# Tokens held step by step in a decoder step kernel, with the first GLU weights split in halves after the state-space loop

## The chip, the cores and the metric

One Trainium2 chip, one of its cores. The metric is the device time of one execution in microseconds (us). The engines are TensorE (PE, with its weight loads as PEld), VectorE (DVE), ScalarE (ACT), GpSimd (POOL) and SyncE (SP, which here only issues transfers).

## The reference

The kernel does one step of a two-layer decoder for 256 prompt tokens and 8 samples of 4 tokens each (288 tokens, width 1024). Layer 0 mixes with latent attention over a paged cache and gated linear attention, layer 1 with an S5 state-space layer. Cut to what the change touches:

```python
# layer 0
h = x + ab_mixer(rmsnorm(x, g_ab)) @ w_out            # residual add
h = h + squared_relu_mlp(rmsnorm(h, g_mlp0))
h = h + sigmoid(rmsnorm(h, g_ple0) @ w_gate) * (p0 @ w_proj)
# layer 1: S5
n = rmsnorm(h, g_c)                                   # "norm 3" in the kernel
u = n.reshape(l, 64 groups, 16)
x_t = lam * x_{t-1} + Bbar u_t                        # a complex state of 64 per group, scanned over t
y = Re(C x) + d * n
zg = gelu(y) @ w_glu
h = h + zg[:, :1024] * sigmoid(zg[:, 1024:])
h = h + squared_relu_mlp(rmsnorm(h, g_mlp1))
h = h + sigmoid(rmsnorm(h, g_ple1) @ w_gate) * (p1 @ w_proj)
```

## The kernel before

**Layout.** Activations lie transposed: channels on the partitions, the 288 tokens along the free dimension, in 8 blocks of 128 channels (`h3[:, b]` is block b of the residual `hT`, `n3` the normalised one). In the program before the tokens stand in their own order, prompt first and then the samples. The S5 layer works on 72 groups of TS = 4 consecutive tokens (J = 72, of which 64 are prompt and 8 are samples), so there every reader takes "step i of group j", which in this layout is every fourth token: `shifted` (L1137 to L1147), which puts the four steps of a block on four groups of 32 partitions, and the `permuted` add in `gated` (L1953).

**Precision.** Most weight matrices are split on the chip into two fp32r parts: ScalarE copies the high part (`hi_unit`, L1284), VectorE subtracts it from the weights to get the low part (`lo_unit`, L1632, 128x2048 elements), and the activations are split likewise (`n_hi_half` at L1557, `n_lo` at L1636). A block is then three matmuls (L750, L751, L752). The other matrices are multiplied in plain fp32 (L769). A unit of 2048 columns streams into a ring of five buffers.

**Order.** Every engine's order is written out by hand. `plan()` gives each PSUM result a bank; a result waits until all readers of the bank's last result are through. Four banks (0 to 3) are handed round to "main" results, four (4 to 7) to "side" results.

**The places of the change.** After the layer-0 MLP, `lag_products` makes the S5 kernel matrices `("G", 0..7)` in two groups of four, in one go; behind them stand the last two blocks (6, 7) of the sums of squares of norm 2. VectorE copies each G (L2055), ScalarE takes three shifted copies of it (L1507) after VectorE's. `ple(0)` follows: for each i of 8, `proj`, `gate` (16 instructions of L769), transposes `("BT", n)` of the S5 matrices (L1137), one block of the sums of squares of norm 3 (L724), and from i = 5 on `shifted(i - 5)` (L1146). When the last sum is there, ScalarE makes the reciprocal root (L1524 on 288 tokens, then L1527, four instructions that pick each step's 72 values for its 32 partitions), and VectorE scales the inputs by it (L2073).

Then the S5 loop, bound together over three engines: per i VectorE turns the inputs (L2085, L2086), scans (L2101), turns back (L2107) and writes the states (L2113, L2114); TensorE makes the inputs (L1192) and the outputs (L1200, and L1206 and L1207 once the states are there); ScalarE applies the GELU (L1550). Inside VectorE's loop, at its i = 6 and 7, stand the low parts that the GLU matrices need first:

```python
                if i == 6:
                    for b in range(4):
                        n_lo(2, b, glu_nhi)
                    lo_unit(U["glu0"])
                if i == 7:
                    lo_unit(U["glu1"])
```

TensorE's GLU begins with blocks 0 to 3 of units glu0 and glu1, then blocks 4 to 7 of both, then glu2 to glu7.

Of the kernel before, what the change touches and what calls it, by code (L numbers as in the profile page):

```python
# [20 lines left out]
P = 128  # L21
# [39 lines left out]
def lay(sizes):  # L61

    at, out = 0, {}
    for name, n in sizes:
# [18 lines left out]
                ("a2", FB * T), ("coef", 20 * 32), ("rsi", J)])  # L83
# [20 lines left out]
def turns(i):  # L104

    return range(3 * i, min(3 * i + 3, 16))


def plan():
# [88 lines left out]
    side("oa")  # L198
    for i in range(8):
        main(("out", i))  # L200
    for L in range(2):
        if L == 1:
            g.add(("ss", 3), "side", 4, 7)
# [26 lines left out]
        g.add(("ss", 2 + 3 * L), "side", 1, 7)  # L230
# [11 lines left out]
def program(nc, ins, outs):  # L242
    g = plan()
    ctx = ExitStack()
    with ctx:
# [59 lines left out]
        bc = lambda ap, shape: ap.broadcast_to(shape)  # L305

# [141 lines left out]
        rsi = s5("rsi")  # L448
# [4 lines left out]
        def sems(names):  # L453
# [12 lines left out]
         hi_ready, unit_split, n_hi, n_split, a_hi, a_split, p_hi, p_split, gate_ready, pool_step, rotation_ready, turned_back, d_ready, x_ready, samples_in, wfin_ready) = sems(  # L466
# [4 lines left out]
            "hi_ready unit_split n_hi n_split a_hi a_split p_hi p_split gate_ready pool_step rotation_ready turned_back d_ready x_ready samples_in wfin_ready")  # L471
# [71 lines left out]
        def _(sp):  # L543
# [28 lines left out]
            sp.wait_ge(table2_in, 16)  # L572
            sp.wait_ge(main_ready, g.of["kpss"][2])
# [131 lines left out]
        def _(pe):  # L705
# [14 lines left out]
            def sumsq_part(k, b):  # L720
# [3 lines left out]
                mm = pe.matmul(ps[:, 0:T], o1024, sq3[:, b % 4], start=b == 0, stop=b == DB - 1)  # L724
# [355 lines left out]
            def mlp(L):  # L1080
# [26 lines left out]
                lag_products()  # L1107
                sumsq_part(2, 6)
                sumsq_part(2, 7)

            def lag_products():
# [3 lines left out]
                for first in (0, 4):  # L1115
                    banks = [bank(("G", first + k)) for k in range(4)]
                    for s in range(4):
                        for bm, cm in ((Bre, Cre), (Bim, Cim)):
                            for k in range(4):
                                blk = 4 * (first + k) + s  # L1120
                                pe.matmul(banks[k][32 * k:32 * k + 32, P * s:P * s + P], bm[:, blk, 3], cm[:, blk, 0:4].rearrange("p i c -> p (i c)"),
                                          start=s == 0 and bm is Bre, stop=False, skip_group_check=True)
                    if first == 0:
                        pe.wait_ge(d_ready, 2)
                    for s in range(4):
                        for k in range(4):
                            mm = pe.matmul(banks[k][32 * k:32 * k + 32, P * s:P * s + 32], ident[0:32, 0:32], diag_d[0:32, 4 * (first + k) + s],
                                           start=False, stop=s == 3, skip_group_check=True)
                            if s == 3:
                                ready(mm, ("G", first + k))  # L1130
# [9 lines left out]
            def shifted(i):  # L1140
# [80 lines left out]
            def glu_pieces(i, lo, hi, wait=None):  # L1221

                w = split_unit(f"glu{i}")
# [7 lines left out]
            for i in range(2, 8):  # L1231
# [1092 lines left out]
```

## Time and profile before

| | |
|---|---|
| median of 3 runs | 1150.16 us (1148.03 to 1151.51) |
| profiled execution: its time / span in the trace | 1150.72 us / 1149.0 us |
| TensorE busy | 1065.5 us, 93% of the span |
| VectorE / ScalarE / GpSimd busy | 544.2 / 413.1 / 140.2 us |
| TensorE busy from 808.0 to 817.5 us | 0.43 us |
| mean granted clock of TensorE | 0.941 of full |

The span is what the trace shows between the first and the last instruction; the profiled execution's own time has 1.7 us around it. A granted clock of 1.00 is 2.4 GHz and 0.50 is 1.2 GHz. A busy TensorE is not one that is at its peak: its instructions overlap. Where it stands idle in the middle of the program, the engine that it waits for sets the time.

### The profile page before, as it was taken

The page shows a single profiled execution, that of the slowest core. Times are in us where ns is not written, and L with a number is a line of the kernel's source. Part 1 is how long each engine was busy: PE and PEld are TensorE (multiplying, and loading weights), DVE is VectorE, ACT ScalarE, POOL GpSimd, SP SyncE. Part 2 cuts the span into 40 slices and gives each one's busy share as a digit, 9 for nine tenths or more (in the row PEclk, how much of TensorE's full clock was granted, in tenths as well). Part 3 has the DMA queues.
Part 4 walks back from the last instruction along what each step waited for, and adds up shares of the span by engine and source line. Part 5 has one row for each costly group of instructions (what it writes and reads, how often), then busy time and mean ns, then how long its engine had stood idle before and what let it go on. Part 6 is the DMA issues. An engine that isn't in the chain of part 4 may idle for free.

```text
span 1149.0 us, 16457 instructions
## 1 busy us (share of the span) xinstructions
PE 1065.5 (93%) x6334; PEld 882.1 (77%) x6334; DVE 544.2 (47%) x956; ACT 413.1 (36%) x714; POOL 140.2 (12%) x236
## 2 busy tenths in 40 slices
PE   6998979999999868999999998989599899999988
PEld 5996446566655546999977777758498899999978
DVE  5432665564453322986430004339564665643453
ACT  5423434431122202665140005323454545523253
POOL 3440000000034230000210007800000000000000
PEclk9997979997789979999999999989599999999999
DMA  7546001210235513344432331040044244433431
GB/s 300 169 153 233 5 1 42 69 47 19 92 119 171 151 59 134 111 163 168 147 129 103 134 147 75 1 192 1 1 156 159 89 168 161 170 147 147 157 136 42
DMA packets 33614, 134.08 MB, mean 117 GB/s; under 512 B 5241, under 2 KB 16761, under 8 KB 20994
## 3 DMA queue, kind: packets, MB, share of 16 engines
q1 hardware_dynamic: 26642, 115.53, 28.2%
q0 software_dynamic: 6896, 17.51, 4.6%
q8 instruction: 50, 0.82, 0.3%
q14 instruction: 26, 0.21, 0.1%
HBM read 128.86 MB, written 4.17 MB: 116 GB/s over the span
## 4 chain that ended last, share of the span: by engine, by line
PE 74%; DVE 13%; ACT 6%; issue 5%; POOLq 1%; DMA 1%; POOL 1%; DVEq 0%; ACTq 0%
PE ps L769 17%; PE ps L750 11%; PE ps L751 11%; PE ps L752 11%; PE ps L929 8%; PE ps L724 2%; DVE ring_split L1632 1%; DVE arena L1970 1%; PE ps L932 1%; PE ps L834 1%; DVE nT L1643 1%; PE ps L994 1%; POOLq L597 1%; ACT up_hi_split L1284 1%; PE ps L1037 1%
## 5 line engine op out<-in xcount | busy, mean ns | idle before, releaser
L929 PE MATMUL ps<-arena 128*128 128x512 f32 x256 | 150.8, 681 | 0.0
L769 PE MATMUL ps<-arena,ring 128*128 128x288 f32 x512 | 125.1, 406 | 0.0
L769 PEld LDWEIGHTS ps<-arena,ring 128*128 128x128 f32 x512 | 97.2, 190 | 26.8
L1632 DVE TENSOR_TENSOR ring_split<-ring,hi_split 128x2048 fp32r<-128x2048 f32 x37 | 84.6, 2291 | 53.0 <-ACT hi_split L1284 53.0
L932 PEld LDWEIGHTS ps<-arena 128*128 128x128 f32 x256 | 51.9, 203 | 68.2 <-issue 68.2
L750 PE MATMUL ps<-nhi_split,hi_split 128*128 128x288 f32 x320 | 96.8, 302 | 5.7 <-DVE nT_split L1636 4.6
L751 PE MATMUL ps<-nT_split,hi_split 128*128 128x288 f32 x320 | 95.0, 297 | 0.0
L752 PE MATMUL ps<-nhi_split,ring_split 128*128 128x288 f32 x320 | 94.7, 296 | 0.0
L1261 ACT ACTIVATE sq<-hT 128x288 f32<-128x288 f32 x48 | 20.6, 441 | 184.7 <-DVE hT L1919 150.9
L1919 DVE TENSOR_TENSOR hT<-hT,ps 128x288 f32<-128x288 f32 x24 | 10.9, 454 | 159.0 <-PE ps L769 129.0
L1284 ACT ACTIVATE hi_split<-ring 128x2048 fp32r<-128x2048 f32 x37 | 70.4, 1908 | 35.6 <-DMA ring<-in_stream 35.6
L1752 DVE TENSOR_REDUCE arena<-arena 128x8 f32<-128x512 f32 x64 | 43.5, 685 | 82.7 <-ACT arena L1359 82.7
L750 PE MATMUL ps<-up_nhi_split,up_hi_split 128*128 128x288 f32 x256 | 77.3, 302 | 5.4 <-DVE nT_split L1636 4.3
L751 PE MATMUL ps<-nT_split,up_hi_split 128*128 128x288 f32 x256 | 76.1, 297 | 0.0
L752 PE MATMUL ps<-up_nhi_split,ring_split 128*128 128x288 f32 x256 | 75.8, 296 | 0.0
L750 PE MATMUL ps<-a2hi_split,hi_split 128*128 128x288 f32 x256 | 75.8, 296 | 0.0
L751 PE MATMUL ps<-a2lo_split,hi_split 128*128 128x288 f32 x256 | 75.5, 295 | 0.0
L752 PE MATMUL ps<-a2hi_split,ring_split 128*128 128x288 f32 x256 | 75.3, 294 | 0.0
L1359 ACT ACTIVATE arena<-ps 128x512 f32<-128x512 f32 x64 | 38.0, 595 | 100.8 <-PE ps L929 97.2
L750 PEld LDWEIGHTS ps<-nhi_split,hi_split 128*128 128x128 f32 x320 | 60.5, 189 | 8.7 <-issue 5.2
L769 PE MATMUL ps<-nT,ring 128*128 128x288 f32 x256 | 64.2, 409 | 1.7 <-ACT arena L1507 1.3
L769 PEld LDWEIGHTS ps<-nT,ring 128*128 128x128 f32 x256 | 48.9, 192 | 15.8 <-issue 1.8
(360 smaller groups left out, 2342.2 us busy)
## 6 DMA issues: line engine op xcount, KB each, us to landing
ring<-in_stream SPq DMA_DIRECT2D x97, 1024.0 KB, 5.0
arena<-in_ckvT SPq DMA_DIRECT2D x64, 128.0 KB, 2.0
arena<-in_ckv POOLq DMA_DIRECT2D x49, 128.0 KB, 2.7
arena<-in_wu POOLq DMA_DIRECT2D x1, 2176.0 KB, 11.0
arena<-in_s POOLq DMA_DIRECT2D x4, 512.0 KB, 3.9
out_gla_s<-arena POOLq DMA_DIRECT2D x4, 512.0 KB, 2.9
arena<-in_ckv SPq DMA_DIRECT2D x15, 128.0 KB, 2.7
hT<-in_x SPq DMA_DIRECT2D x2, 576.0 KB, 4.4
```

The lines of the kernel that those rows point to most:

```text
L724: mm = pe.matmul(ps[:, 0:T], o1024, sq3[:, b % 4], start=b == 0, stop=b == DB - 1)
L750: pe.matmul(ps[:, 0:T], wh[:, k, col:col + P], xh, start=first and k == which[0], stop=False)
L751: pe.matmul(ps[:, 0:T], wh[:, k, col:col + P], xl, start=False, stop=False)
L752: mm = pe.matmul(ps[:, 0:T], wl[:, k, col:col + P], xh, start=False, stop=last and k == which[-1])
L769: mm = pe.matmul(ps[base:base + m, 0:T], wv[:, k, col:col + m], rhs(k), start=first and k == 0, stop=last and k == blocks - 1)
L929: mm = pe.matmul(ps[:, :], pages[:, p % 4, j, k], wuk[:, k], start=k == 0, stop=k == KB - 1)
L932: mm = pe.matmul(sc[:, 32 * j:32 * j + 32], pages[:, p % 4, j, k], qabs[:, k, b], start=False, stop=j == 1 and k == KB - 1, skip_group_che ...
L1261: act.activation(sq3[:, b % 4], h3[:, b], ACT.Square).then_inc(sq_ready, 1)
L1284: act.activation(hi_part(v)[:, :], ring[SPLITS[v] % RING][:, :], ACT.Copy).then_inc(hi_ready, 1)
L1359: act.activation(ksq[:, n % 2].rearrange("p h n -> p (h n)"), ps[:, :], ACT.Square).then_inc(bank_of(name), 1)
L1632: V.tensor_tensor(lo_parts[slot][:, :], ring[slot][:, :], as_whole(hi_part(v)[:, :]), ALU.subtract).then_inc(unit_split, 1)
L1752: V.tensor_reduce(ssq[:, (k + j) * NS + b], ksq[:, j], AX.X, ALU.add).then_inc(ksum_ready, 1)
```

## The change

It has five parts.

1. **Tokens step by step.** The residual is kept with token 4j + i at column 72i + j from the output projection on. The attention results are written so (`by_step`), the two p inputs and the output are laid out so outside the kernel, and `x` is loaded a second time in that order (`x_by_step`, 1152 KB) on SyncE's queue between the ring loads and the cache pages; VectorE waits for it before the first residual add. `shifted` and the GLU's add then read and write runs of 72.
2. **Norm-3 sums in four partition groups.** A block's sum is four products of 32 weight columns with 72 tokens, one for each step, into its own 32 partitions of bank 7; the reciprocal root is then two ScalarE instructions of 72.
3. **Lag products in two groups.** G0 to G3 first, then the last two blocks of norm 2's sums, then G4 to G7. ScalarE makes norm 2's root after G1 and no longer after G3, VectorE applies norm 2 after G3 and no longer after G7.
4. **Transposes.** BT0 to BT3 come at i = 0 and three each after it, so that none is left for i = 5; BT0 has bank 7.
5. **GLU low parts in halves, behind the loop.** VectorE's loop holds none of them any more; ScalarE's high parts of glu0 and glu1 move one i later, and the second half of the high activations ahead of the table load.

```diff
 def turns(i):
-    return range(3 * i, min(3 * i + 3, 16))
+    return range(3 * i + 1 if i else 0, min(3 * i + 4, 16))
...
-    side("oa")
+    side("oa", 4)
...
-            g.add(("ss", 3), "side", 4, 7)
+            g.add(("ss", 3), "side", 1, 7)
...
             for i in range(8):
+                if i == 4:
+                    g.add(("ss", 2), "side", 1, 7)
...
-                    g.add(("BT", n), "side", 1, 4 + n % 3)
+                    g.add(("BT", n), "side", 1, 4 + (n + 2) % 3 if n else 7)
...
+            sp.wait_ge(n_ready, DB)
+            sp.dma_start(hT[:, :], ins["x_by_step"]).then_inc(x_again, 16)
             sp.wait_ge(main_ready, g.of["kpss"][2])
...
-                mm = pe.matmul(ps[:, 0:T], o1024, sq3[:, b % 4], start=b == 0, stop=b == DB - 1)
+                if k == 3:
+                    for t in range(TS):
+                        mm = pe.matmul(ps[32 * t:32 * t + 32, 0:J], o1024[:, 0:32], sq3[:, b % 4, J * t:J * t + J], start=b == 0, stop=b == DB - 1,
+                                       skip_group_check=True)
...
-                lag_products()
+                lag_products(0)
                 sumsq_part(2, 6)
                 sumsq_part(2, 7)
+                lag_products(4)
...
-                                   h3[:, b:b + 4].rearrange("p b (j i) -> p b i j", i=TS)[:, :, t], start=True, stop=True, skip_group_check=True)
+                                   h3[:, b:b + 4, J * t:J * t + J], start=True, stop=True, skip_group_check=True)
...
             for i in range(2):
+                pe.wait_ge(glu_first, i + 1)
                 glu_pieces(i, 0, 4, split_wait(2) if i == 0 else None)
             for i in range(2):
+                split_unit(f"glu{i}")
                 glu_pieces(i, 4, 8, split_wait(2) if i == 0 else None)
...
-            for t in range(TS):
-                lo = 32 * t
-                act.activation(rsi[lo:lo + 32, :], rs[lo:lo + 32, :].rearrange("p (j i) -> p i j", i=TS)[:, t], ACT.Exp, scale=-0.5).then_inc(bank_of(("ss", 3)), 1)
+            rsqrt(rsi, ("ss", 3), width=J)
...
                 if i == 4:
                     n_hi_half(0)
+                if i == 5:
                     hi_unit(U["glu0"])
-                if i == 5:
+                if i == 6:
                     hi_unit(U["glu1"])
+            n_hi_half(1)
             table_with_exp_and_ln()
-            n_hi_half(1)
...
-            V.tensor_copy(mix[:, 0:4, TP:T], ps[:, 0:128].rearrange("p (k t) -> p k t", k=4)).then_inc(bank_of("oa"), 1)
+            for k in range(4):
+                V.tensor_copy(by_step(mix[:, k])[:, JP:J], ps[:, TN * k:TN * k + TN].rearrange("p (j i) -> p j i", i=TS)).then_inc(bank_of("oa"), 1)
...
-                if i == 6:
-                    for b in range(4):
-                        n_lo(2, b, glu_nhi)
-                    lo_unit(U["glu0"])
-                if i == 7:
-                    lo_unit(U["glu1"])
+            lo_half(0, 0)
+            for b in range(4):
+                n_lo(2, b, glu_nhi)
+            lo_half(1, 0)
+            lo_half(0, 1)
             for b in range(4, DB):
                 n_lo(2, b, glu_nhi)
+            lo_half(1, 1)
```

**The loop's end on VectorE.** Before, between the states of iteration 6 and the last iteration's end (L2101 is a scan, L1636 `n_lo`, L1632 a low part of a whole unit, L2085 and L2086 the next inputs):

```order
L2101 SCALAR_TENSOR_TENSOR const<-arena,const 128x256 x2
L1636 TENSOR_TENSOR nT_split<-nT,glu_nhi_split 128x288 x4
L1632 TENSOR_TENSOR ring2_split<-ring2,glu_hi0_split 128x2048
L2085 TENSOR_TENSOR const<-ps3,arena 128x2x128
L2086 TENSOR_TENSOR tmp<-ps3,arena 128x2x128
```

The same engine in the changed program, from the last states (L2125, L2126, which were L2113 and L2114) on; L2150 is a low part of half a unit, L1647 is `n_lo`, L1643 the low part of glu2:

```order
L2125 TENSOR_TENSOR arena<-sq 128x4x63
L2126 TENSOR_TENSOR arena<-sq 128x4x63
L2150 TENSOR_TENSOR ring2_split<-ring2,glu_hi0_split 128x1024
L1647 TENSOR_TENSOR nT_split<-nT,glu_nhi_split 128x288 x4
L2150 TENSOR_TENSOR ring3_split<-ring3,glu_hi1_split 128x1024
L2150 TENSOR_TENSOR ring2_split<-ring2,glu_hi0_split 128x1024
L1647 TENSOR_TENSOR nT_split<-nT,glu_nhi_split 128x288 x4
L2150 TENSOR_TENSOR ring3_split<-ring3,glu_hi1_split 128x1024
L1643 TENSOR_TENSOR ring4_split<-ring4,glu_hi2_split 128x2048
```

The scan of iteration 6 is now followed at once by iteration 7, and the low parts stand behind iteration 8's states.

**The lag products on VectorE.** Before (L2055 copies a G out of its bank, L1618 is norm 2, L1948 the first gate's product):

```order
L2055 COPY arena<-ps1 32x512
L2055 COPY arena<-ps2 32x512
L2055 COPY arena<-ps3 32x512
L2055 COPY arena<-ps0 32x512
L2055 COPY arena<-ps4 32x512
L1618 SCALAR_TENSOR_TENSOR nT<-hT,par,rs 128x288 x8
L1948 TENSOR_TENSOR tmp<-tmp,ps1 128x288
```

and in the changed program, where the copy is L2066 and norm 2 is L1629:

```order
L2066 COPY arena<-ps1 32x512
L1629 SCALAR_TENSOR_TENSOR nT<-hT,par,rs 128x288 x8
L2066 COPY arena<-ps2 32x512
L2066 COPY arena<-ps3 32x512
L2066 COPY arena<-ps0 32x512
L2066 COPY arena<-ps4 32x512
L1961 TENSOR_TENSOR tmp<-tmp,ps1 128x288
```

Norm 2 now stands ahead of the copies of G4 (bank 2) to G7 (bank 4).

**The first shifted block on TensorE.** Before, at i = 5 of `ple(0)` (L769 is the gate, L1137 the transposes BT15, L724 the sum, L1146 `shifted(0)`):

```order
L769 MATMUL ps0<-nT,ring0 128x288 x8
L1137 MATMUL ps4<-const,arena 128x128 x4
L724 MATMUL ps7<-sq,ones 128x288
L1146 MATMUL ps4<-hT,const 32x288 x4
L769 MATMUL ps1<-pT,ring2 128x288 x2
```

and in the changed program, where they are L780, L732, L1157 and L780:

```order
L780 MATMUL ps0<-nT,ring0 128x288 x8
L732 MATMUL ps7<-sq,ones 32x72 x4
L1157 MATMUL ps4<-hT,const 32x288 x4
L780 MATMUL ps1<-pT,ring2 128x288 x2
L780 MATMUL ps2<-nT,ring1 128x288 x8
```

No transposes stand ahead of the shifted block any more, and its bank 4 was last used one i earlier.

## Rows read from the trace of the kernel before

**Rows 1.** Page, busy time: us, share of the span, instructions.
```profile
PE 1065.5 (93%) x6334; PEld 882.1 (77%) x6334; DVE 544.2 (47%) x956; ACT 413.1 (36%) x714; POOL 140.2 (12%) x236
```
**Rows 2.** Waits of PE: total us, times, longest us.
```profile
PE ps L1206 <- DVE arena L2114: 14.2, 3, 9.2
```
**Rows 3.** Windows of PE: us, busy (instructions), granted clock, DMA share, GB/s.
```profile
746.80:749.00 2.20, 2.20 (x9) 0.50 0.00 0
...
808.00:817.50 9.50, 0.43 (x2) 0.50 0.00 0
...
827.00:830.40 3.40, 3.39 (x16) 0.50 0.00 0
...
835.00:838.00 3.00, 3.00 (x24) 0.99 0.00 0
```
**Rows 4.** Timeline, loop's end: start, duration us, [idle before <- releaser].
```profile
805.07 1.27 DVE L2101 TENSOR_TENSOR_SCAN const<-arena,const 128x256 f32<-128x256 f32 x2
...
808.52 1.56 DVE L1636 TENSOR_TENSOR nT_split<-nT,glu_nhi_split 128x288 fp32r<-128x288 f32 x4 [2.19 <-ACT glu_nhi_split L1557]
...
813.53 0.42 DVE L2085 TENSOR_TENSOR const<-ps,arena 128x256 f32<-128x256 f32 x1
...
817.39 1.27 DVE L2101 TENSOR_TENSOR_SCAN const<-arena,const 128x256 f32<-128x256 f32 x2
...
817.62 0.67 PE L1206 MATMUL ps<-arena 128*128 128x71 f32 x2 [9.19 <-DVE arena L2114]
...
820.64 1.91 ACT L1284 ACTIVATE glu_hi_split<-ring 128x2048 fp32r<-128x2048 f32 x1
...
822.57 1.67 ACT L1550 ACTIVATE nT<-ps 32x288 f32<-32x288 f32 x4
822.58 2.29 DVE L1632 TENSOR_TENSOR ring_split<-ring,glu_hi_split 128x2048 fp32r<-128x2048 f32 x1 [3.92 <-ACT glu_hi_split L1284]
824.79 1.29 DVE L2107 TENSOR_TENSOR sq<-const,arena 128x512 f32<-128x512 f32 x2
...
826.45 0.41 DVE L2114 TENSOR_TENSOR arena<-sq 128x252 f32<-128x252 f32 x1
...
830.42 0.59 PE L750 MATMUL ps<-glu_nhi_split,glu_hi_split 128*128 128x288 f32 x1
```
**Rows 5.** Timeline, low part of glu2 and the first GLU result.
```profile
836.98 2.29 DVE L1632 TENSOR_TENSOR ring_split<-ring,glu_hi_split 128x2048 fp32r<-128x2048 f32 x1 [1.24 <-ACT glu_hi_split L1284]
...
842.20 0.69 DVE L2160 TENSOR_TENSOR arena<-arena,sq 128x512 f32<-128x512 f32 x1
...
842.36 0.41 ACT L1448 ACTIVATE tmp<-ps 128x288 f32<-128x288 f32 x1 [5.41 <-PE ps L752]
...
844.32 0.70 DVE L1953 TENSOR_TENSOR hT<-hT,tmp 128x288 f32<-128x288 f32 x1
```
**Rows 6.** Timeline, end of the first embedding stage.
```profile
745.68 1.20 PE L1146 MATMUL ps<-hT,const 128*32 128x288 f32 x8 [2.23 <-DVE arena L2063]
...
746.81 2.29 PE L769 MATMUL ps<-pT,ring 128*128 128x288 f32 x4
...
754.90 1.24 PE L769 MATMUL ps<-pT,ring 128*128 128x288 f32 x4
...
763.78 0.50 ACT L1524 ACTIVATE rs<-ps,eps 128x288 f32<-128x288 f32 x1 [0.84 <-PE ps L724]
764.32 1.37 ACT L1527 ACTIVATE arena<-rs 32x72 f32<-32x72 f32 x4
```
**Rows 7.** Timeline, lag products and the first gate.
```profile
696.15 2.83 DVE L2055 COPY arena<-ps 32x512 f32<-32x512 f32 x4 [1.01 <-PE ps L1127]
696.95 4.76 ACT L1507 ACTIVATE arena<-ps 32x384 f32<-32x384 f32 x12 [2.67 <-DVE arena L2055]
...
704.98 3.50 DVE L1618 SCALAR_TENSOR_TENSOR nT<-hT,par,rs 128x288 f32<-128x288 f32 x8
705.65 4.12 PE L769 MATMUL ps<-nT,ring 128*128 128x288 f32 x16 [1.33 <-ACT arena L1507]
```

More of the change, by code:

```diff
@@ L229, in plan @@
                     main(("G", i), 4)
-        g.add(("ss", 2 + 3 * L), "side", 1, 7)
+        else:
+            g.add(("ss", 5), "side", 1, 7)
         for i in range(8):
@@ L1106, in mlp, with lag_products @@
                         sumsq_part(2, i - 2)
-                lag_products()
+                lag_products(0)
                 sumsq_part(2, 6)
                 sumsq_part(2, 7)
-            def lag_products():
+                lag_products(4)
+            def lag_products(first):
                 pe.wait_ge(b_copied, 16)
                 pe.wait_ge(c_copied, 20)
[L1115 to L1125, printed above, removed]
-                        for k in range(4):
[L1127 to L1130, printed above, removed]
@@ new lines, in lag_products @@
+                banks = [bank(("G", first + k)) for k in range(4)]
+                for s in range(4):
+                    for bm, cm in ((Bre, Cre), (Bim, Cim)):
+                        for k in range(4):
+                            blk = 4 * (first + k) + s
+                            pe.matmul(banks[k][32 * k:32 * k + 32, P * s:P * s + P], bm[:, blk, 3], cm[:, blk, 0:4].rearrange("p i c -> p (i c)"),
+                                      start=s == 0 and bm is Bre, stop=False, skip_group_check=True)
@@ L1132, in b_turned @@
+                if first == 0:
+                    pe.wait_ge(d_ready, 2)
+                for s in range(4):
+                    for k in range(4):
+                        mm = pe.matmul(banks[k][32 * k:32 * k + 32, P * s:P * s + 32], ident[0:32, 0:32], diag_d[0:32, 4 * (first + k) + s],
+                                       start=False, stop=s == 3, skip_group_check=True)
+                        if s == 3:
+                            ready(mm, ("G", first + k))
             def b_turned(i):
@@ L1261, in square, with rsqrt @@
                     act.activation(sq3[:, b % 4], h3[:, b], ACT.Square).then_inc(sq_ready, 1)
-            def rsqrt(out, name, rows=P, scale=1.0):
+            def rsqrt(out, name, rows=P, scale=1.0, width=T):
                 ps = result(act, name)
-                link(act.activation(out, ps[0:rows, 0:T], ACT.Ln, scale=scale, bias=eps[0:rows, :]))
+                link(act.activation(out, ps[0:rows, 0:width], ACT.Ln, scale=scale, bias=eps[0:rows, :]))
                 act.activation(out, out, ACT.Exp, scale=-0.5).then_inc(bank_of(name), 1)
@@ L1913, in _ @@
             ps = result(dve, "oa")
-            V.tensor_copy(mix[:, 0:4, TP:T], ps[:, 0:128].rearrange("p (k t) -> p k t", k=4)).then_inc(bank_of("oa"), 1)
+            for k in range(4):
+                V.tensor_copy(by_step(mix[:, k])[:, JP:J], ps[:, TN * k:TN * k + TN].rearrange("p (j i) -> p j i", i=TS)).then_inc(bank_of("oa"), 1)
             def add_to_h(names, at=0):
@@ L1938, in up_split, with gated @@
                     V.tensor_tensor(a2lo[:, i - 1], a2[:, i - 1], as_whole(a2hi[:, i - 1]), ALU.subtract).then_inc(a_split, 1)
-            def gated(base, values, gates, permuted=False, unit_of=None, after=None):
+            def gated(base, values, gates, unit_of=None, after=None):
                 for i in range(8):
@@ L2160, in _ @@
             V.tensor_tensor(vs, vs, xt[:, :, 1], ALU.add).then_inc(states_ready, 1)
-            gated(8, [("glu_a", i) for i in range(8)], [("glu_g", i) for i in range(8)], permuted=True, unit_of=lambda i: U[f"glu{i}"])
+            gated(8, [("glu_a", i) for i in range(8)], [("glu_g", i) for i in range(8)], unit_of=lambda i: U[f"glu{i}"])
             norm_split(4, prm("g_mlp1"), 3)
@@ L2278, in arrays @@
     r = {
-        "const": constants(), "param": par, "x": blocks(x.T), "stream": np.stack(stream),
+        "const": constants(), "param": par, "x": blocks(x.T), "x_by_step": blocks(by_step(x).T), "stream": np.stack(stream),
         "table": a["page_table"].reshape(1, -1),
         "wu": np.concatenate(wu, 1),
-        "p": np.stack([blocks(np.concatenate([a["p_prompt"][i][0], a["p_sample"][i].reshape(TN, -1)], 0).T) for i in range(2)]),
+        "p": np.stack([blocks(by_step(np.concatenate([a["p_prompt"][i][0], a["p_sample"][i].reshape(TN, -1)], 0)).T) for i in range(2)]),
         "kpeT": a["cache_kpe"][0].transpose(0, 2, 1),
@@ L2314, in tokens @@
         return m.reshape(-1, b, T).transpose(2, 1, 0).reshape(T, -1)
[L2316 removed]
+    y, ckv, kpe = tokens(got["y"], DB).reshape(TS, J, D).transpose(1, 0, 2).reshape(T, D), tokens(got["ckv"], KB), got["kpe"].T
     c = np.ascontiguousarray
```

40 lines of the change are left out of this document (24 added, 16 removed).

## The prediction

> **What bounds the kernel now.** I read the page first. TensorE is busy for 93% of the span and VectorE for 47% [rows 1], so a change pays where TensorE stands idle, or where its clock is low. The list of TensorE's waits puts one place far ahead: the last products of the S5 loop (L1206) wait 14.2 us for VectorE's states (L2114), 9.2 us of it at once [rows 2]. The windows show the price a second time: from 808.0 to 817.5 TensorE is busy for 0.43 us and its granted clock is 0.50 (1.2 GHz), it is still 0.50 in the window up to 830.4, in which the engine works all the time, and is back at full only from 835 on [rows 3].
>
> The timeline says why [rows 4]. VectorE ends the scan of iteration 6 at 805.07 + 1.27 = 806.3. It then waits 2.19 us for ScalarE, does four `n_lo` and the low part of glu0, which waits too, and begins iteration 7 only at 813.53. That ends with the scan at 817.39 + 1.27 = 818.7. Next VectorE waits 3.92 us for ScalarE's high part of glu1, splits it, and turns back the last states from 824.79 on, until 826.45 + 0.41 = 826.9. So of the 20.5 us behind the scan of iteration 6, 7.2 and 6.1 us are the GLU's preparation, most of it waiting. TensorE's GLU begins at 830.42.
>
> **The change part by part.**
>
> *GLU low parts behind the loop.* I follow the changed order with the durations of rows 4. Iteration 7 takes 818.7 - 813.5 = 5.1 us and starts at 806.3: scan done at 811.5. The last turning back and states take 826.9 - 824.8 = 2.1 us: done at 813.6. ScalarE's next steps wait for that scan: its small copies, then the GELU of y5(5), 1.67, until 813.5; high part of glu0, 1.91, until 815.4; GELU of y5(6) until 817.0; high part of glu1 until 818.9; GELU of y5(7) until 820.6; the four high activations, about 1.5 like `n_lo`, until 822. VectorE waits for glu0 until 815.4, does its half (2.29 for 2048 columns; a little over half of that for 1024, 1.2) until 816.6, and the first `n_lo` (1.56/4) until 817.0. That is the earliest start of the GLU.
>
> TensorE has y5(6) and y5(7) before it. y5(6)'s states come 1.3 us ahead of the scan, at 810.2. At low clock a block's 16 products take 3.4 us [rows 3]; with the eight products of y5(7) between them (1.9 for eight at that clock, half of 16 and a little more) TensorE is through at 818.9, at full clock at 815.4. So the GLU starts between 817.0 and 818.9: 11.5 to 13.4 us earlier.
>
> What is late next? VectorE's other half units and `n_lo` end at 818.9 + 1.2 + 1.2, then 1.5 behind ScalarE's last high activation, then 1.2: about 824. The high part of glu2 comes behind the table load at about 825, its low part until 827.5, and the final states, which took 842.20 + 0.69 - 839.27 = 3.6 us before [rows 5], until 831.1. Only then can the first GLU result leave its bank for glu2: 831.6. Before, glu_g0 was complete at 842.36 [rows 5] and the other 24 products of glu1 follow it at 0.13 us each (24 instructions in 3.0 us [rows 3]), so glu2 began at 845.5, 15.1 after the GLU's start. Now that is 817.0 + 15.1 = 832.1, just behind VectorE's 831.6, and about 833 if y5 comes late, since then more of the slow stretch lies ahead of the GLU. I take 845.5 - 832.5 = **-13.0 us**, bounds -11.5 and -14.
>
> *No transposes at i = 5.* `shifted(0)` waits 2.23 us until VectorE has emptied bank 4 of BT15 [rows 6]. The wait goes: bank 4 was last filled one i earlier, 6 us before. Behind it `proj` takes 2.29 us against 1.24 one i later, at a granted clock of 0.50 [rows 3, 6]: 1.05, and the gate behind it loses a little too. The moved transposes cost the same at i = 0. **-3.5 us**, bounds -2.2 and -3.8.
>
> *Root of norm 3.* L1524 and L1527 take from 763.78 to 764.32 + 1.37 = 765.7, 1.9 us in which all wait [rows 6]. Two instructions of 72 at the price of one of the four L1527 (0.34) are 0.7. **-1.2 us**, bounds -0.9 and -1.4.
>
> *Runs of 72 instead of every fourth token.* `shifted` takes 1.20 us for four products of 32 columns, the full-width `proj` 1.24 for two of the same length [rows 6]. If the stride is what keeps the four from running side by side, each is 0.6 cheaper. Those at i = 5 and 6 lie on TensorE's path, the third lies beside the last gate, the rest beside VectorE's loop. Between 0 and -1.2, in the middle: **-0.6 us**. The Trainium skill (SBUF — State Buffer, the note on cachelines) says that reads which cross into a new 16-byte line each time pay a penalty; every fourth fp32 value is just that. No row before shows the run for comparison; by the rule the sum would take the whole -1.2. The GLU's permuted add takes 0.70 where 0.45 is usual, and only the last one is waited for [rows 5]: **-0.2 us**.
>
> *Norm-3 sums in four groups.* A block's sum was one product of 288 (about 0.55, half of L769's 1.24 for two); `shifted`'s price scaled to 72 tokens is 0.3, four in a row without overlap are 0.55, and a pause on each side of a change of width may come on top. I take **0**, bounds -0.3 and +0.5 for each of the seven blocks that lie in TensorE's path, -2 to +3.5.
>
> *Lag products.* The gate's first instruction waits for ScalarE to empty G4's bank [rows 7]. Now: VectorE copies G0 to G3 until 699.0; ScalarE is through with G1 at 696.95 + 6 x 0.40 = 699.3 and makes the root until 700.3 (0.97, as before); norm 2 takes 3.50, until 703.9; then VectorE's copy of G4, 0.71, until 704.6; then ScalarE's three copies, 1.2: 705.9 against 705.65. Norm 2 comes 4.6 us earlier, but it was not what the gate waited for, and G4's copies now queue behind it. TensorE stands idle in smaller pieces (ahead of the second group, of `proj`, of the gate), which could lower its clock. **+0.3 us**, bounds 0 and +2.
>
> *Attention result.* The last copy before the output projection becomes four on its waiting path. A VectorE instruction of 252 elements takes 0.41 [rows 4], and these have 32: **+0.3 us**, bounds 0 and +1.2. The other strided writes are not waited for. The second load of x stands on SyncE's queue ahead of the cache pages, which wait there for TensorE's `kpss` in any case, and is needed only at the first residual add, long after: 0.
>
> **Sum.** -13.0 - 3.5 - 1.2 - 0.6 - 0.2 + 0 + 0.3 + 0.3 = -17.9. The profiled execution took 1150.72 us (span 1149.0 and 1.7 around it): 1132.8. It is 0.56 above the median of the runs, 1150.16; from that it is 1132.3. I say **1132.5**.
>
> **The rivals.**
>
> *The half units come late.* If ScalarE's chain slips (its high part of glu0 now stands behind the scan and a GELU), or the low clock lasts 8 us into the GLU, the first term is -9 and the time 1136.5. For it: VectorE waited for exactly this engine twice, 2.19 and 3.92 us [rows 4], and the clock stayed low through busy work up to 835 [rows 3]. Against: ScalarE's steps fit one behind the other above with nothing between. 12%.
>
> *The four-group sums cost.* At the upper bound, +3.5: 1136. The Trainium skill (TensorEngine Tiling (Array Packing), Key Properties) says that a change of tiling mode drains TensorE; each block now changes it twice. The trace has `shifted` in that mode, 1.20 us for four products with its first pause in it, which leaves room for tenths of a us and not more [rows 6]. 10%.
>
> *The clock gives more.* If the shorter pauses around the root of norm 3 and in the loop's end keep the clock at full, the first S5 products and y5(6), y5(7) and the GLU's start gain another 4 us: 1128.5. 10%.
>
> *Slower.* One mechanism: the four-group products do not overlap at all, and each pays a pause of its own. At 1 us apiece the 32 of them cost 32 - 4.4 = 28 us: 1160. It decides from (17.9 + 4.4)/32 = 0.7 us apiece; `shifted`'s four together take 1.20. 3%. *No change*: the same at 0.7 us, or VectorE and ScalarE so changed at the loop's end that the waits merely move: 1150, 2%.
>
> **How the numbers follow.** The forecast has 63%, with a range of its own from 1128.5 to 1136. With the rivals at 1136.5, 1136 and 1128.5 and their own spread, 1127 to 1140 leaves out less than 2 in 10. A measurement of this kernel tells about 0.3% (3.5 us) from no change. Faster 0.95, same 0.02, slower 0.03.
>
> **What would show it.** VectorE goes from the scan of iteration 6 to iteration 7 without a pause, and the last states come about 7 us after that scan, not 20. TensorE's longest wait for L2126 is about 2 us. Its GLU starts 10 to 12 us behind that scan, not 24. No wait of `shifted` for L2075. Two root instructions of some 0.3 us. The first gate still waits for ScalarE's copies of G4. Wrong it would be if TensorE waited for VectorE's half units inside the GLU, if each sum block of norm 3 took over 0.8 us, or if the stages ahead of 690 us, which I leave as they are, had moved.

## The result and the profile after

The changed kernel takes 1156.89 us (median of 20 runs, 1150.74 to 1158.53), the kernel before 1148.95 (20 runs, 1143.25 to 1151.86). The ratio is 1.007 with a 95% interval of 1.0056 to 1.0084: slower by 6.4 to 9.7 us, where 17.9 us less were forecast. The profiled execution has a span of 1154.6 us.

On the page of the changed kernel, the line of busy times answers to [rows 1]:

```profile
PE 1087.2 (94%) x6382; PEld 906.5 (79%) x6382; DVE 545.4 (47%) x961; ACT 412.8 (36%) x711; POOL 138.0 (12%) x236
```

TensorE is busy for 21.7 us more, with 48 instructions more. Its largest wait of before, L1206 for L2114 [rows 2], has no row any more under its new numbers (L1217, L2126). So the waits went as forecast, and the time came back as busy time.

Windows of TensorE in the changed kernel (us, busy and instructions, granted clock, DMA share, GB/s):

```profile
745.00:757.00 12.00, 12.00 (x85) 1.00 0.27 86
757.00:762.00 5.00, 1.29 (x24) 1.00 1.02 423
762.00:765.00 3.00, 3.00 (x18) 0.52 1.01 426
765.00:770.00 5.00, 5.00 (x32) 0.50 0.54 223
...
775.00:785.00 10.00, 10.00 (x52) 0.50 0.01 2
...
825.00:835.00 10.00, 10.00 (x49) 0.50 0.00 0
835.00:845.00 10.00, 10.00 (x58) 0.72 0.01 2
```

The same stretch of the kernel before:

```profile
765.00:770.00 5.00, 3.51 (x20) 0.68 1.01 424
770.00:775.00 5.00, 5.00 (x32) 0.64 0.16 67
775.00:785.00 10.00, 10.00 (x84) 1.00 0.01 2
785.00:795.00 10.00, 10.00 (x88) 1.00 0.01 2
```

Both kernels come into the S5 loop (at 766.49 before, 761.55 now) at half clock. Before, the clock is back at full by 775, and TensorE issues 84 to 88 products in 10 us. Now it stays at 0.50 (1.2 GHz) through the whole loop, and 49 to 52 are issued in 10 us, while the engine shows busy without a pause. The loop's end, as a timeline of the changed kernel (L1211 is `outputs`, L2113 the scan, L2150 a half low unit):

```profile
807.23 1.27 DVE L2113 TENSOR_TENSOR_SCAN const<-arena,const 128x256 f32<-128x256 f32 x2
...
812.09 3.62 PE L1203 MATMUL ps<-arena 128*128 128x72 f32 x16
...
815.76 1.27 DVE L2113 TENSOR_TENSOR_SCAN const<-arena,const 128x256 f32<-128x256 f32 x2
...
824.29 0.43 DVE L2104 TENSOR_TENSOR const<-const,tmp 128x256 f32<-128x256 f32 x1 [4.61 <-ACT arena L1543]
...
825.63 1.27 DVE L2113 TENSOR_TENSOR_SCAN const<-arena,const 128x256 f32<-128x256 f32 x2
...
828.88 1.91 ACT L1298 ACTIVATE glu_hi_split<-ring 128x2048 fp32r<-128x2048 f32 x1
830.83 1.23 DVE L2150 TENSOR_TENSOR ring_split<-ring,glu_hi_split 128x1024 fp32r<-128x1024 f32 x1 [1.81 <-ACT glu_hi_split L1298]
830.86 1.92 PE L1211 MATMUL ps<-arena 128*128 128x72 f32 x8
831.97 1.56 DVE L1647 TENSOR_TENSOR nT_split<-nT,glu_nhi_split 128x288 fp32r<-128x288 f32 x4
...
835.94 0.59 PE L761 MATMUL ps<-glu_nhi_split,glu_hi_split 128*128 128x288 f32 x1
```

The scans are 8.5 and 9.9 us apart, where the kernel before had 5.2 to 5.4 between most of them (799.90 to 805.07 the last such pair), and now VectorE waits for what TensorE makes (4.61 us at once; the row names ScalarE, which had itself waited 3.58 us for TensorE shortly before). A block of 16 input products takes 3.62 us (1.98 at full clock, in a row of e5 below). VectorE's half unit and first `n_lo` are ready at about 832.4; the GLU begins at 835.94, when TensorE has finished y5(7).

To compare kernels whose earlier stages shift in time, I read two lengths: from the last `ss` product pair ahead of the lag products to the first product of the S5 inputs (**up to the loop**), and from there to the GLU's first product (**the loop**). Before: 693.14 to 766.49 is 73.35 us, and to 830.42 is 63.93. Changed: 692.25 to 761.55 is 69.30, and to 835.94 is 74.39. So the changed kernel gains 4.05 us up to the loop and loses 10.46 in it, 6.4 in all. The first GLU result leaves its bank at 847.90 (842.36 before [rows 5]), which is again 6.4 later; behind 845 both show 273.9 us busy in 283. The whole loss lies in the loop.

Of the signs that the prediction gave, VectorE does go from the scan of iteration 6 to iteration 7 without a pause (817.03 to 817.07). But its last states come 12.0 us behind that scan (829.0) and not 7, and the GLU begins 18.9 us behind it and not 10 to 12.

The two lengths are each from one trace. Where the same early code stands unchanged, the first of them begins anywhere from 688.0 (e12 below) to 698.6 us (e4), and from the GLU's first product to the end the traces take 315.9 to 319.0 us. So the terms of the change that lie ahead of the first length (the attention result) or behind the loop (the GLU's add) are not measured here, and where a profiled run lies 5 to 9 us off its median (e3, e4, e9 and e12), most of that is in where the first length begins.

### The profile page after: what moved, and what is told of

The parts are those of the page before. It is cut to its first block, busy times and chain, and to the rows that moved or that the text cites. A ratio compares the mean times of both kernels' runs of the same rounds, so it can differ in the third digit from the quotient of the medians.

```text
span 1154.6 us, 16558 instructions
## 1 busy us (share of the span) xinstructions
PE 1087.2 (94%) x6382; PEld 906.5 (79%) x6382; DVE 545.4 (47%) x961; ACT 412.8 (36%) x711; POOL 138.0 (12%) x236
## 4 chain that ended last, share of the span: by engine, by line
PE 81%; DVE 8%; ACT 5%; issue 4%; POOLq 1%; DMA 1%; POOL 1%; DVEq 0%; ACTq 0%
PE ps L780 17%; PE ps L761 12%; PE ps L763 12%; PE ps L762 12%; PE ps L940 7%; PE ps L1203 2%; PE ps L735 1%; PE ps L1211 1%; PE ps L1218 1%; PE ps L1217 1%; PE ps L943 1%; PE ps L845 1%; PE ps L1005 1%; POOLq L603 1%; ACT up_hi_split L1298 1%
## 5 line engine op out<-in xcount | busy, mean ns | idle before, releaser
L780 PE MATMUL ps<-arena,ring 128*128 128x288 f32 x512 | 125.1, 406 | 0.0
L780 PEld LDWEIGHTS ps<-arena,ring 128*128 128x128 f32 x512 | 97.2, 190 | 26.8
L1643 DVE TENSOR_TENSOR ring_split<-ring,hi_split 128x2048 fp32r<-128x2048 f32 x37 | 84.6, 2292 | 55.4 <-ACT hi_split L1298 55.4
L780 PE MATMUL ps<-nT,ring 128*128 128x288 f32 x256 | 66.6, 420 | 2.5 <-issue 1.9
L780 PEld LDWEIGHTS ps<-nT,ring 128*128 128x128 f32 x256 | 50.2, 197 | 17.4 <-issue 2.3
## 6 DMA issues: line engine op xcount, KB each, us to landing
arena<-in_wu POOLq DMA_DIRECT2D x1, 2176.0 KB, 10.4
```

Of the source, the lines that this page charges most:

```text
L780: mm = pe.matmul(ps[base:base + m, 0:T], wv[:, k, col:col + m], rhs(k), start=first and k == 0, stop=last and k == blocks - 1)
L1643: V.tensor_tensor(lo_parts[slot][:, :], ring[slot][:, :], as_whole(hi_part(v)[:, :]), ALU.subtract).then_inc(unit_split, 1)
```

## The experiments

My theory after the traces: `shifted`, read in one run, takes half as long at full clock (0.67 for 1.20 us), TensorE's work around the loop's entry becomes thinner, and the clock no longer comes back. Rivals: the four-group sums keep the clock low (a row width of 72 tokens, one more mode of the array); the GLU halves or the lag split do; or the entry's waits alone decide.

Each ratio is to the kernel before, run beside the variant. The table is told first, since the runs speak to each other; "loop" is the length defined above (63.93 before, 74.39 changed).

| run | median us | ratio, 95% | loop us |
|---|---|---|---|
| e1 no layout | 1138.25 | 0.992 (0.9899 to 0.9941) | 53.86 |
| e2 GLU halves only | 1140.17 | 0.9927 (0.9902 to 0.9952) | 53.50 |
| e3 strided read | 1135.16 | 0.9891 (0.9873 to 0.9909) | 53.60 |
| e4 full sums | 1157.3 | 1.009 (1.0071 to 1.0109) | 74.89 |
| e5 products of ones at entry | 1138.68 | 0.9902 (0.9867 to 0.9936) | 58.72 |
| e6 `shifted` twice | 1135.32 | 0.9871 (0.9843 to 0.9898) | 53.80 |
| e7 blocks fastest | 1137.71 | 0.9937 (0.9897 to 0.9977) | 53.57 |
| e8 before, in one run | 1166.66 | 1.0155 (1.0124 to 1.0186) | 83.77 |
| e9 e6, lag in one go | 1130.48 | 0.9842 (0.9824 to 0.986) | 53.69 |
| e10 e9, ones at the end | 1129.11 | 0.983 (0.9812 to 0.9847) | 52.53 |
| e11 lag split only | 1154.61 | 1.0051 (1.0035 to 1.0068) | 63.91 |
| e12 two blocks twice | 1135.96 | 0.9893 (0.9876 to 0.9911) | 54.71 |

**e1 and e2: parts of the change on the kernel before.** e1 takes the lag split, the moved transposes and the GLU halves, and leaves the layout by step and the four-group sums out. e2 takes the GLU halves alone:

```diff
-                    lo_unit(U["glu0"])
-                if i == 7:
-                    lo_unit(U["glu1"])
...
+            lo_half(0, 0)
+            for b in range(4):
+                n_lo(2, b, glu_nhi)
+            lo_half(1, 0)
+            lo_half(0, 1)
...
+            lo_half(1, 1)
```

> The kernel before with three of the five parts: lag products in two groups, the new places of the transposes, and the GLU's low parts in halves behind the loop. Tokens in their own order, norm-3 sums as one full-width product, as before. The trace of the changed kernel shows TensorE at 1.2 GHz from 762 to 841 us, through the whole S5 loop. Theory A (the every-fourth-token reads of the shifted products are what let the clock come back early in the loop before): the clock is full in most of the loop, time about 1150.7 - 13 - 3.5 = 1134 to 1138. Theory B (the clock falls and stays down because the work ahead of the loop or its moment has moved): could be either, 1134 or 1155. Theory C (the missing low parts at the loop's end pull it down): low clock at the end, 1150 or more.

> The kernel before with the GLU's low parts in halves behind the loop, and nothing else of the change. The loop up to iteration 6 is that of before, so by theories A and B its clock is full, and the forecast's first term shows alone: 13 us less, 1136 to 1139. Theory C (the part itself brings the low clock): 1150 or more, with 0.50 in windows of the loop.

Both are faster than before, so the loss sits in what e1 leaves out. (One of e2's six runs took 3268 us and is left out of the ratio.) The loop of e2 is 10.4 us shorter than before's; its ratio makes it 8.4 us (5.5 to 11.3). Its timeline at the loop's end shows why not 13:

```profile
807.37 1.42 ACT L1560 ACTIVATE glu_nhi_split<-nT 128x288 fp32r<-128x288 f32 x4
808.82 0.28 ACT L1536 ACTIVATE arena<-ps 128x32 f32<-128x32 f32 x2
...
810.54 1.27 DVE L2105 TENSOR_TENSOR_SCAN const<-arena,const 128x256 f32<-128x256 f32 x2
...
815.73 1.22 DVE L2142 TENSOR_TENSOR ring_split<-ring,glu_hi_split 128x1024 fp32r<-128x1024 f32 x1 [1.81 <-ACT glu_hi_split L1287]
816.88 1.56 DVE L1640 TENSOR_TENSOR nT_split<-nT,glu_nhi_split 128x288 fp32r<-128x288 f32 x4
...
819.30 0.59 PE L750 MATMUL ps<-glu_nhi_split,glu_hi_split 128*128 128x288 f32 x1
```

ScalarE's high activations (807.37) stand ahead of its last small copies (L1536), for which VectorE's last iteration waits: the last scan comes 6.2 us behind the one before it (804.38), not 5.2. VectorE is ready at 817.3; the GLU begins two us later, behind y5(7) at half clock.

**e3: the strided read put back** in the changed kernel.

```diff
-                                   h3[:, b:b + 4, J * t:J * t + J], start=True, ...
+                                   h3[:, b:b + 4].rearrange("p b (j i) -> p b i j", i=TS)[:, :, t], start=True, ...
```

> The changed kernel, but its shifted products read every fourth column of the residual as those before did. Since the columns now stand in another order, it computes the S5 layer on the wrong tokens; the amount of work is the same. Theory A: the clock comes back within some 8 us of the loop's start as before, and the time falls to 1133 to 1138. Theory B: the loop stays at 0.50, 1155 to 1158, and the three shifted products ahead of the loop cost 0.5 us more each.

One line takes the ratio from 1.007 to 0.9891, some 21 us. A window of e3, then its entry into the loop: the last norm-3 sum, `shifted` as the clock is low, the next 16 input products, `shifted` at full clock:

```profile
775.00:785.00 10.00, 10.00 (x88) 1.00 0.01 2
```
```profile
756.66 0.33 PE L732 MATMUL ps<-sq,ones 128*32 128x72 f32 x8 [1.70 <-ACT sq L1275]
...
762.07 1.22 PE L1157 MATMUL ps<-hT,const 128*32 128x288 f32 x8
...
763.22 2.68 PE L1203 MATMUL ps<-arena 128*128 128x72 f32 x16
...
765.83 1.20 PE L1157 MATMUL ps<-hT,const 128*32 128x288 f32 x8
```

The clock is back within the second 16 input products (2.68 us, where they take 3.69 in the changed kernel). Up to there only one strided block has run inside the loop, and at half clock it took 1.22 us, where the one in a run takes 1.19. So inside the loop the strided read has added next to no time when the clock returns. What it has lengthened are the three blocks ahead of the loop, at full clock (1.20 for 0.67 us each); behind the third of them TensorE's pause ahead of the last sum is 1.70 us here and 2.22 in the changed kernel.

**e4: full-width sums of norm 3** in the changed kernel (99 is never reached), with a root of five instructions.

```diff
-                if k == 3:
+                if k == 99:
...
-            rsqrt(rsi, ("ss", 3), width=J)
...
+            link(act.activation(rs[:, :], ps[:, 0:T], ACT.Ln, bias=eps[:, :]))
+            for t in range(TS):
+                lo = 32 * t
+                act.activation(rsi[lo:lo + 32, :], rs[lo:lo + 32, J * t:J * t + J], ACT.Exp, scale=-0.5)...
```

> The changed kernel, but norm 3's sums are one full-width product a block again and the reciprocal root is five ScalarE instructions again. Theory A: the loop stays at 0.50, 1156 to 1159. Theory B (less TensorE work just ahead of the loop, the four-group sums 0.33 us where full-width ones took 0.65, is what pulls the clock down at 762): the clock stays or comes back, 1134 to 1140.

No gain: 1157.3, and the loop is at half clock as before e4's edit (74.89 us). The stretch up to the loop grows from 69.30 to 71.60 us (698.61 to 770.21), so the group sums and the short root save 2.3 us. The rival that the group sums are to blame is out.

**e5: TensorE kept busy at the entry**, by three products of ones (128x512) around the last norm-3 sum.

```diff
+            keep_busy(2)
             sumsq_part(3, 7)
+            keep_busy(1)
```

> The changed kernel with three added full-width products of 512 columns of ones (0.85 us each at full clock), two ahead of the last block of norm 3's sums and one behind it, where TensorE waited 2.2 and 1.5 us before the loop. Their result is overwritten. Theory A1 (the loop holds the full clock once it enters with it, as it did before from 787 to 807 us with no shifted product left in it; what is lost is only the return from the low level): the clock is at full in the loop and the time falls to 1130 to 1136. Theory A2 (the loop with contiguous reads is too thin to hold the full clock wherever it begins): the clock falls a few us later all the same, 1155 to 1158.

TensorE enters the loop at full clock, and 18 us of the loss are gone. But the clock falls in the loop's middle. Timeline of e5:

```profile
779.15 1.11 PE L1218 MATMUL ps<-arena 128*128 128x72 f32 x8 [0.90 <-DVE arena L2092]
...
782.36 1.98 PE L1210 MATMUL ps<-arena 128*128 128x72 f32 x16 [0.31 <-ACT arena L1550]
...
785.41 1.11 PE L1218 MATMUL ps<-arena 128*128 128x72 f32 x8 [1.08 <-DVE arena L2092]
...
787.03 0.54 PE L1225 MATMUL ps<-arena 128*128 128x71 f32 x2
787.36 0.64 PE L1224 MATMUL ps<-arena 128*128 128x71 f32 x2
```

Having entered fast it runs ahead of VectorE, and waits four times between 762 and 787 (the first, 0.43 us, ahead of the loop's first product); a pair of 71 then takes 0.64 instead of 0.39. In the kernel before from 775 to 800 and in e12 from 770 to 796, where the clock stays at full, TensorE's list has no wait at all. Once down at 787, the clock does not come back before 824.

**e6: every `shifted` block made twice** in the changed kernel, the second time over the first. Were the stride needed for something other than the time that it takes, this would change nothing.

```diff
+                for _ in range(2):
                     for t in range(TS):
                         mm = pe.matmul(ps[32 * t:32 * t + 32, 0:4 * J], ...
```

> The changed kernel, but each shifted block is made twice into the same bank, so that it takes about 1.2 us at full clock as the strided ones did, with contiguous reads. If time spent in shifted products is what brought the clock back, it comes back: 1133 to 1139. If it is the stride itself, the loop stays at 0.50 and takes up to 8 x 1.2 us more: 1158 to 1167.

More work makes the kernel some 22 us faster (1.007 to 0.9871). Window and timeline of e6:

```profile
770.00:775.00 5.00, 5.00 (x57) 1.00 0.01 2
```
```profile
766.04 2.15 PE L1158 MATMUL ps<-hT,const 128*32 128x288 f32 x16
...
770.41 1.18 PE L1158 MATMUL ps<-hT,const 128*32 128x288 f32 x16
```

The doubled block takes 1.18 us at full clock, as much as the strided one. So no stride is needed to bring the clock back. But at half clock it takes 2.15 us, where the strided one took 1.22: e6 adds work inside the loop as well, and e3 did not. It doesn't show that the strided read works in the same way.

**e7: blocks as the fastest dimension**, a strided read of the same tokens.

```diff
-                                   h3[:, b:b + 4, J * t:J * t + J], ...
+                                   h3[:, b:b + 4, J * t:J * t + J].rearrange("p b j -> p j b"), ...
```

> The changed kernel, computing the right thing, but the shifted products read their 288 columns with the four blocks innermost (a stride of 1152 bytes) and VectorE takes them out of the bank in that order. If any strided read does what every fourth column did in the third kernel (1135.2 us), the clock comes back and the time is 1133 to 1140. If it was the data or the wrong tokens of that kernel, the loop stays at 0.50 and the time is 1156 to 1160.

e7 reads the right tokens and gains nearly as much as e3, so e3's wrong tokens are not the cause. Eight of its twelve runs took 1135.6 to 1142.2 us at a mean clock of 0.94, four 1151.0 to 1153.2 at 0.92, the mean clock of the changed kernel (the median is of all twelve, the ratio leaves out the three slowest). Both outcomes in one kernel: the return of the clock hangs on little. That is a reading of the mean clocks, since the profile is of a run of the first group.

**e8: the mirror of e3**, the read in one run put into the kernel before.

```diff
-                                   h3[:, b:b + 4].rearrange("p b (j i) -> p b i j", i=TS)[:, :, t], ...
+                                   h3[:, b:b + 4, J * t:J * t + J], ...
```

> The mirror of the third kernel: the kernel before, but its shifted products read runs of 72 columns, so it computes the S5 layer on the wrong tokens, with the same amount of work. If the stride is the cause, this one edit brings the low clock to the whole loop and makes the kernel before slower: 1165 to 1175 (1147.5 + the 24 us that the changed kernel's loop lost). If the cause needs the rest of the change, 1145 to 1148.

Again the S5 layer gets the wrong tokens. This line alone costs the kernel before 1.55%, 17.8 us. Window of e8, where before had 1.00:

```profile
775.00:785.00 10.00, 10.00 (x52) 0.50 0.00 1
```

One thing goes with the outcome in these traces and is tried alone in none of them, TensorE's pause ahead of the last norm-3 sum. It is 1.36 us in the kernel before, in e1, e2 and e11, 1.70 in e3 and 1.73 in e7, and there the clock returns; it is 1.87 in e4 and e8 and 2.22 in the changed kernel, and there it doesn't. A strided block just ahead of the pause is longer and leaves less of it. So the strided read may act by the blocks ahead of the loop, and not by those inside it; a run with only the one or only the other is missing.

**e9 and e11: the lag split**, undone in e6 and put alone into the kernel before.

```diff
-                lag_products(0)
+                lag_products()
                 sumsq_part(2, 6)
                 sumsq_part(2, 7)
-                lag_products(4)
```

> The kernel with each shifted block made twice (1135.3 us, ratio 0.987), with the change's third part undone: lag products in one go, norm 2's last sums behind them, ScalarE's root after G3 and norm 2 after G7, as before. In the changed kernel's trace the first gate's 16 products start 0.3 us later behind the lag products than before and take 6.99 us at 1.2 GHz against 4.12. Theory L1 (the split costs what those rows show, by the idle pieces that it makes ahead of the gate): the gate takes 4.1 us again and the time is 3 us less, about 1132, ratio 0.984. Theory L2 (the low clock there is chance): the same time within 1 us, and 7 us again for the gate.

> The kernel before with the third part alone (lag products in two groups, norm 2's last sums between them). Theory L1: the first gate starts 0.3 us later and runs at 1.2 GHz for most of its 16 products, 2 to 3 us slower than the kernel before, ratio 1.002 to 1.003. Theory L2: the same time, and a gate of 4.1 us.

The split costs 0.51% alone (0.35 to 0.68). Undoing it takes e6's ratio from 0.9871 to 0.9842, whose intervals overlap; the traces show the gain more surely, 67.10 us up to the loop (698.30 to 765.40) instead of 70.30 (692.15 to 762.45), and a gate of 4.12 us again. The first gate of e11, then that of the changed kernel with what comes ahead of it (compare [rows 7], 4.12 us):

```profile
706.97 7.12 PE L772 MATMUL ps<-nT,ring 128*128 128x288 f32 x16 [2.03 <-issue]
```
```profile
697.37 1.95 PE L1132 MATMUL ps<-arena 128*32 128x128 f32 x64 [1.03 <-ACT arena L1521]
...
703.06 2.83 DVE L2066 COPY arena<-ps 32x512 f32<-32x512 f32 x4
...
705.10 6.99 PE L780 MATMUL ps<-nT,ring 128*128 128x288 f32 x16 [1.92 <-issue]
```

In the kernel before a stretch of low clock falls on the second group of lag products, which takes 3.43 us where it takes 1.95 above. The split doesn't create such a stretch, it moves it onto the gate:

```profile
698.25 3.43 PE L1121 MATMUL ps<-arena 128*32 128x128 f32 x64 [2.20 <-ACT arena L1507]
```

**e10: products of ones at the loop's end** of e9, three ahead of y5(6)'s wait and one ahead of the GLU.

```diff
+                if i == 6:
+                    keep_busy(("glu_a", 0), 3)
                 pe.wait_ge(samples_in, i + 1)
...
+            keep_busy(("glu_a", 0), 1)
```

> The kernel of the run before this one, with full-width products of 512 columns of ones where TensorE waits at the loop's end: three ahead of the wait of y5(6), one ahead of the GLU. Their results are overwritten. If the clock in the GLU's first 10 us hangs on the work of the waits as it did at the loop's entry, it stays at full past 803 us, y5(6), y5(7) and the GLU's first products gain up to 4 us: 1128, ratio 0.981. If it falls all the same, the added products cost up to 2 us: 1134.

It is the fastest version, 1.7% below the kernel before (1.53 to 1.88), but its interval overlaps e9's. Windows of e9 and of e10 ahead of the GLU:

```profile
812.00:820.00 8.00, 8.00 (x39) 0.50 0.00 0
```
```profile
809.00:814.00 5.00, 5.00 (x42) 1.00 0.00 0
```

The clock falls all the same at 801.7 (granted 0.54 from 804 to 809, while the three products of ones run) and is back by 809. So y5(7) now runs at full clock, the loop is 1.2 us shorter, and from the GLU's first product to its first result it takes 10.2 us (814.11 to 824.30) instead of 11.5 (819.09 to 830.63).

**e12: only the first two `shifted` blocks of the loop made twice** in the changed kernel.

```diff
+                for _ in range(2 if i in (3, 4) else 1):
```

> The changed kernel with only the first two shifted blocks of the loop made twice (number 3 and 4), the rest once. If what counts is that the clock is brought back once, early in the loop, it then stays at full until the waits at the loop's end: 1134 to 1138. If contiguous shifted blocks let it fall again, as it fell at 787 in the run with products of ones ahead of the loop, there is a second stretch of 0.50 in the loop: 1138 to 1150. If two are too few to bring it back: 1156 to 1159.

As good as all eight within the intervals, and here nothing ahead of the loop differs from the changed kernel (the pause ahead of the last norm-3 sum is 2.23 us). So products inside the loop can do it alone. Windows of e12:

```profile
765.00:770.00 5.00, 5.00 (x39) 0.69 0.00 2
770.00:775.00 5.00, 5.00 (x50) 1.00 0.00 0
775.00:785.00 10.00, 10.00 (x93) 1.00 0.01 2
```

Once the clock is back it stays, with the same single blocks behind that the changed kernel has. So these same blocks run the rest of the loop at half clock in one kernel and at full clock in the other, and in this pair the two doubled blocks at the entry decide. They don't always: e5 entered at full clock and lost it.

## Why the prediction was wrong

**The step that failed** is *Runs of 72 instead of every fourth token*, put at -0.6 us. The edit did what the step says of its duration: `shifted` takes 0.67 instead of 1.20 at full clock. The timeline of the changed kernel at the end of the first embedding stage (compare [rows 6]) shows it with the other terms of that stage:

```profile
745.10 0.33 PE L732 MATMUL ps<-sq,ones 128*32 128x72 f32 x8
745.25 0.67 PE L1157 MATMUL ps<-hT,const 128*32 128x288 f32 x8
745.85 1.24 PE L780 MATMUL ps<-pT,ring 128*128 128x288 f32 x4
...
759.74 0.33 PE L732 MATMUL ps<-sq,ones 128*32 128x72 f32 x8 [2.22 <-ACT sq L1275]
760.13 0.32 ACT L1280 ACTIVATE rs<-ps,eps 128x72 f32<-128x72 f32 x1 [0.45 <-PE ps L732]
760.49 0.26 ACT L1281 ACTIVATE rs<-rs 128x72 f32<-128x72 f32 x1
...
761.55 3.15 PE L1203 MATMUL ps<-arena 128*128 128x72 f32 x16 [1.48 <-DVE arena L2085]
764.63 1.19 PE L1157 MATMUL ps<-hT,const 128*32 128x288 f32 x8
```

What it left out is that the kernel before leans on the strided read for its clock: without it the clock stays at 1.2 GHz through the loop. The price is 21 us: the loop takes 74.39 us in the changed kernel and 53.6 in e3, which differs by this one line; e8 shows the sign and size the other way round (+17.8). By which way the read brings the clock back, the blocks ahead of the loop or something else in the stride, stays open. Behind this lies a wider slip: I took every duration of the loop at the clock that the trace of before showed, and looked for low clock only behind long waits. A window of [rows 3] spoke against that (3.39 us busy in 3.40 and still at 0.50), and I read it as a delay, not as a course that can go on.

**GLU halves**, -13.0 forecast (-11.5 to -14): 10.4 in e2's trace, outside my bounds by 1.1 (8.4 by e2's ratio). The mechanism was right. The two missed pieces are ScalarE's order (1 us) and y5(7) at half clock, which ended behind VectorE's work.

**Transposes and bank 4**, -3.5 (-2.2 to -3.8): e1 needs 72.93 us up to the loop (690.49 to 763.42) and e11, which differs there by the transposes alone, 76.76 (694.00 to 770.76): -3.8. The wait of 2.23 us is gone, and `proj` behind it takes 1.24 instead of 2.29.

**Root and four-group sums**, -1.2 and 0: together -2.3 by e4. The root takes 760.13 to 760.75, 0.6 us instead of 1.9; the sum of a block takes 0.33, where it takes 0.65 at full width (e4, at 763.83), and not the 0.55 that I put down as half of 1.24, which is 0.62. The rival that these sums cost was wrong in sign.

**Lag products**, +0.3 (0 to +2, for the clock): +3.4 up to the loop, by e11 (76.76) against before (73.35). The wait moved as forecast, the gate starting 0.34 us later behind the first lag product than before (12.27 for 11.93). The missing 3 us are the gate's own: 6.99 against 4.12 us, since the clock falls as it begins (granted 0.58 from 705 to 712). The text named this, and bounded it too low.

**The slower case**, 3%, had another mechanism (products that do not overlap), which the rows refute. That the time came out slower was not for a reason I had listed. The rival *the clock gives more* had the right subject and the wrong sign.

The sum with measured terms: 4.05 us gained up to the loop, about 10.4 in it, 21 lost: +6.4 in the traces, against +7.9 between the medians.

## What to carry to other kernels

Where TensorE stands close to the pace of another engine, ask of every edit that makes its products cheaper what its clock will do; the busy share won't tell, so read the granted clock of each stage before and after, and try the edit alone, since one such line can eat all that the others win. If a stretch runs at half clock and its products are short, a few superfluous products at its entry are a cheap probe, and may be the cure.

## What the runs showed of the hardware

- TensorE stayed at 1.2 GHz in every window from 765 to 835, 70 us, while its rows show work without a pause. The Trainium skill (TensorE: Matmul & The Clock Gate, HAM oscillation — how this bites in real kernels) ties the low clock to pauses. The fall at the entry agrees with it (1.29 us busy of 5.00 ahead of it). The same page (the Trainium skill, What's actually happening) says that the clock gate goes by how busy TensorE has been of late. If busy as the trace shows it were what counts, the clock would have come back in the loop's first iterations, as in e3; the 70 us don't agree with that, and the measurement decides.
- Redundant products made the changed kernel faster by about 21 us (e6, e12).
- Reading every fourth fp32 value costs at full clock (1.20 for 0.67 us), and almost nothing at half clock (1.22 for 1.19). The Trainium skill (SBUF — State Buffer, Specifications, the note on cachelines) gives a penalty per line crossed, and the trace agrees at full clock alone.
- Open: what the chip counts. In e3 and in the changed kernel the blocks inside the loop take the same time at half clock, and only in e3 does the clock return. That added products can bring it back is shown by e6 and e12; that the strided read does it in the same way, and by which quantity, is not.
- Open as well: why e5's clock fell at 787. The four short waits ahead of it are all that the trace shows, and no run here takes them away alone.
